# Feed-forward gate and up products computed feature-major, with the weights stationary

## Chip, cores and metric

One core of a Trainium2 chip runs the whole program. The metric is the device time of one execution in microseconds; the profile is one execution taken by the hardware profiler. A difference of 0.2% is about what can be told apart for this kernel.

## What is computed

Two layers of a decoder trunk over x of 256 rows and 1024 features, in float32. Each layer is a token mixer and a feed-forward, each followed by a layer norm. The change touches the feed-forward alone:

```python
def _swiglu(x, w_gate, w_up, w_down):
    hid = jax.nn.silu(jnp.einsum('bsd,df->bsf', x, w_gate)) * jnp.einsum('bsd,df->bsf', x, w_up)
    return jnp.einsum('bsf,fd->bsd', hid, w_down)
```

w_gate and w_up are 1024 x 2816, w_down is 2816 x 1024, one set per layer.

## The kernel before

**Precision.** Every large product is made of three fp32r matmuls: with each operand split into hi (its fp32r rounding) and lo (the rest), a x w is xh*wh + xh*wl + xl*wh. ScalarE casts the hi part, VectorE subtracts for the lo part.

**Weights.** They come as pieces of 128 x 2048 (some smaller) into 3 raw slots by the SP queue (L790); ScalarE casts a piece to one of 5 w_hi slots (L897, step "hi"), VectorE makes w_lo (L1034, step "lo"). The cast of piece i waits until the matmuls of piece i-5 are done; the load of piece i waits for the lo split of piece i-3. A gate-and-up piece holds four blocks of 128 input features, each with 256 columns of w_gate and 256 of w_up side by side. A down piece holds 256 rows of w_down.

**Rows and tiles.** The 256 rows are two tiles t of 128. A matmul has one 128 x 128 stationary operand and one moving operand. In "mm" (L1292 to L1303) the stationary is a block of activations, feature-major (`hi["act"]`, `lo["act"]`, 8 blocks x 256 rows), and the moving operand is the weights, up to 512 columns; the product comes out row-major, in one PSUM bank of 512 columns.

**Order.** `write_plan` writes one list of steps, and each engine runs through the list and issues the steps that concern it, in that order. `mm` puts the splits of coming weight pieces ahead of each step of matmuls: one "lo" step, and one "hi" step for each piece that earlier matmuls have freed.

**Feed-forward.** It has 11 chunks c of 256 hidden features, counted from 0 here. `gate_up` runs, for one tile and one half of the input features, 4 blocks x 3 terms = 12 matmuls of 512 columns: 256 gate columns and 256 up columns. When both halves are done, the step "hidden" takes silu of the gate columns on ScalarE (L1003) and multiplies by the up columns on VectorE (L1140), into `act_fns`. These hidden values are row-major, but as stationary operand of the down product they are needed feature-major. So `turn_hid` transposes them on TensorE, two 128 x 128 blocks per tile (L1312), ScalarE casts the result to `hi["y"]` (L901) and VectorE subtracts for `lo["y"]` (L1041). `down` then runs 2 output halves x 2 blocks x 3 terms = 12 matmuls of 512 columns per tile, accumulated over the chunks in four banks. `y` has 6 block slots, two for each of three chunks.

The order of chunk c for c from 2 to 10: gate and up over input half 0 for both tiles; the two turns of chunk c-1 (for c over 2); input half 1 for both tiles; then, for c up to 8, the down product of chunk c-1. The down products of chunks 8, 9 and 10 come last, tile by tile, and the turns of chunk 10 lie between them (L542 to L549):

```python
for t in range(TT):
    for c in range(FFN_CHUNKS - HELD, FFN_CHUNKS):
        if t == 0 and c > last - TT:
            turn_hid(last, c - last + TT - 1)
```

After them follow the layer norm and the next layer, whose first weight pieces are split meanwhile.

Of the kernel before, what the change touches and what calls it, by code (L numbers as in the profile page):

```python
# [21 lines left out]
F32 = mybir.dt.float32  # L22
F32R = mybir.dt.float32r
I32 = mybir.dt.int32
ALU = mybir.AluOpType
ACT = mybir.ActivationFunctionType

P = 128
# [40 lines left out]
QUARTERS = 4  # L69
STAGES = 2  # L70
FFN_CHUNKS = D_FF // 256


def layer_pieces(layer, w):
# [59 lines left out]
def write_plan(orders, base):  # L134
# [13 lines left out]
    def turn(src, buf, k0, nk, t, dst, dst_k0, ready):  # L148

        use = aux_bank()  # L150
        plan.append(("turn", src, buf, k0, nk, t, dst, dst_k0, use, ready, count.next("turn")))
        return use
# [6 lines left out]
    def split_hi():  # L159
        i = split_next[0]  # L160
        if i < total:
            plan.append(("hi", i, release.get(i - HI_SLOTS)))
            lo_waiting.append(i)
            split_next[0] += 1
# [24 lines left out]
    release = {}  # L189
    attending = [False]  # L190

    def mm(i, t, lhs, outs, frees, lhs_ready, full=()):

        if half_split and half_split[0] <= i:
            finish_lo()
        while lo_waiting and lo_waiting[0] <= i:
            split_lo()
        if attending[0]:
            start_lo()
        else:  # L200
            split_lo()
        if freed[0]:
            freed[0] -= 1
            split_hi()
        plan.append(("mm", i, t, lhs, outs, frees and not full, lhs_ready, full))
        if frees:
            release[i] = ("filled", full[-1]) if full else ("used", count.next("used"))
            freed[0] += 1
# [64 lines left out]
    for layer, order in enumerate(orders):  # L273
# [222 lines left out]
        def gate_up(c, t, half, use, frees):  # L496
            mm(at[("gu", c, half)], t, ("act", ACT_SLOTS[half]), [(use, 0, NW, half == 0, half == 1)],
               frees, turned[t, half], (use,) if half else ())
            if half:
                hid[c, t] = use  # L500
                plan.append(("hidden", c, t, use, count.next("hid")))

        def turn_hid(c, t):
            turned["h", c, t] = turn("hid", c % 2, 0, 2, t, "y", 2 * (c % 3), ("bank", hid[c, t]))

        down_use = {t: None for t in range(TT)}
# [22 lines left out]
        turn_hid(1, 1)  # L529
        for c in range(2, FFN_CHUNKS):  # L530
            use = [gu_bank() for _ in range(TT)]
            for t in range(TT):
                gate_up(c, t, 0, use[t], t == TT - 1)
            if c > 2:
                for t in range(TT):
                    turn_hid(c - 1, t)
            for t in range(TT):
                gate_up(c, t, 1, use[t], t == TT - 1)
            if c < FFN_CHUNKS - HELD + 1:
                for t in range(TT):  # L540
                    down(c - 1, t, t == TT - 1)
# [28 lines left out]
def trunk(nc, d):  # L570
# [9 lines left out]
    with ExitStack() as ctx:  # L580
# [3 lines left out]
        def sem(name):  # L584
            return ctx.enter_context(nc.semaphore(name))
# [92 lines left out]
        exp_done = sem("exp_done")  # L678
        summed = sem("summed")
        silu_done = sem("silu_done")  # L680
        merge_done = sem("merge_done")
        x_ready = sem("x_ready")
        mean_ready = sem("mean_ready")
# [33 lines left out]
        def weights(ring, i, n_rows):  # L717
            _, nk, cols = pieces[i]
            return ring[slot_of(i, n_rows)][:, 0:nk * cols]

        def wait_lo(engine, i):

            engine.wait_ge(lo_done, 2 * (i + 1))
# [150 lines left out]
        def _(act):  # L874
# [10 lines left out]
            for step in PLAN:  # L885
# [60 lines left out]
                elif kind == "scores" and not (step[1]["b"] == 1 and step[1]["t"]) or kind == "scores2":  # L946
                    u = step[1]
                    for e, (b, n) in enumerate(u["s2"] or u["s"]):
                        slot = 2 * (u["u"] % 4) + e
                        pr = prob[u["t"]][e][:, 0:(GROUPS if u["b"] == 1 else 1) * u["w"]]  # L950
                        act.wait_ge(drained[b], n)
                        act.activation(pr, pr, ACT.Exp, bias=neg_max[:, slot:slot + 1], scale=-1.0,  # L952
                                       accum_out=denom[:, slot:slot + 1]).then_inc(exp_done, 1)
                elif kind == "turn_p":
                    u = step[1]
                    b, n = u["pt"]
                    act.wait_ge(filled[b], n)
                    t = u["t"]
                    act.copy(prob_t[:, t:2 * t + 1, :], group_view(bank[b], t + 1, 2 * P)).then_inc(drained[b], 1)
                elif kind == "weigh":  # L960
                    u = step[1]
                    if u["b"] == 1:
                        act.wait_ge(summed, u["sum_n"])
                    act.wait_ge(inverse_done, u["weigh_n"])
                    for e in range(2):
                        slot = 2 * (u["u"] % 4) + e
                        pr = prob[u["t"]][e][:, 0:u["w"]]
                        ins = act.activation(pr, pr, ACT.Identity, scale=rdenom[:, slot:slot + 1])  # L968
                    ins.then_inc(weighed, 1)
                elif kind == "values":  # L970
                    _, u, _, _ = step
                    b, n = u["o"]
                    act.wait_ge(filled[b], n)
                    act.copy(hi["y"][:, Y_SLOTS[u["b"]][u["p"]], :], bank[b][:, 0:SEQ]).then_inc(y_hi_done, 1)
                elif kind == "gate":
                    _, nh, t, (b, n), last_merge = step
                    act.wait_ge(filled[b], n)
                    if last_merge is not None:
                        act.wait_ge(merge_done, last_merge)
                    act.activation(act_fn[2 * nh + t][:, :], bank[b][:, :], ACT.Tanh, scale=0.5).then_inc(drained[b], 1)  # L980
                elif kind == "spread_rows":
                    act.wait_ge(norms_loaded, 16)
                    act.wait_ge(rows_zeroed, 2)
                    act.copy(w_hi[HI_SLOTS - 1][0:4, 0:NW + 4], norm_rows).then_inc(rows_hi_done, 1)
                elif kind == "turn_rows":
                    _, t, k0, nk, (b, n) = step
                    act.wait_ge(filled[b], n)
                    act.copy(merged[t][:, k0 * P:(k0 + nk) * P], bank[b][:, 0:nk * P]).then_inc(drained[b], 1)
                elif kind == "split_rows":
                    t = step[1]  # L990
                    for b, n in first_turns[t]:
                        act.wait_ge(drained[b], n)
                    act.copy(hi["act"][:, :, t * P:(t + 1) * P], group_view(merged[t], KT, P)).then_inc(first_hi, 1)
                elif kind == "statistics":
                    for t, _ in step[1]:
                        means += 1
                        act.wait_ge(mean_ready, means)
                        act.activation(squares_out, x[t][:, :], ACT.Square, bias=neg_mean[:, t:t + 1],  # L998
                                       accum_out=square_sum[:, t:t + 1]).then_inc(squares_ready, 1)
                elif kind == "hidden":  # L1000
                    _, c, t, (b, n), _ = step
                    act.wait_ge(filled[b], n)
                    act.activation(act_fn[2 * (c % 2) + t][:, 0:256], bank[b][:, 0:256],  # L1003
                                   ACT.Silu).then_inc(silu_done, 1)

        @block.vector
        def _(dve):
# [19 lines left out]
            for step in PLAN:  # L1027
# [93 lines left out]
                elif kind == "merge":  # L1121
# [6 lines left out]
                    if br == 0:  # L1128
                        dve.scalar_tensor_tensor(out=out, in0=sig, scalar=1.0, in1=bank[b][:, :],
                                                 op0=ALU.add, op1=ALU.mult).then_inc(drained[b], 1)  # L1130
                    else:
                        dve.scalar_tensor_tensor(out=sig, in0=sig, scalar=1.0, in1=bank[b][:, :],
                                                 op0=ALU.add, op1=ALU.mult).then_inc(drained[b], 1)
                        dve.wait_ge(drained[b], n)
                        dve.tensor_tensor(out, out, sig, ALU.add).then_inc(merge_done, 1)
                elif kind == "hidden":
                    _, c, t, (b, n), idx = step
                    dve.wait_ge(silu_done, idx)
# [96 lines left out]
        def _(pe):  # L1235
# [9 lines left out]
            for step in PLAN:  # L1245
# [36 lines left out]
                if kind == "mm":  # L1282
                    _, i, t, (lhs, slots), outs, frees, (lb, ln), full = step
                    _, nk, cols = pieces[i]
                    pe.wait_ge(first_split if lb == "rows" else drained[lb], ln)
                    wait_lo(pe, i)
                    wh = weights(w_hi, i, HI_SLOTS).rearrange("p (k n) -> p k n", k=nk)
                    wl = weights(w_lo, i, HI_SLOTS).rearrange("p (k n) -> p k n", k=nk)
# [3 lines left out]
                    for o, (use, c0, width, start, stop) in enumerate(outs):  # L1292
# [7 lines left out]
                        if use in full:  # L1300
                            ins.then_inc(filled[use[0]], 1)
                    if frees:
                        ins.then_inc(piece_used, 1)  # L1303
                elif kind == "turn":
                    _, src, buf, k0, nk, t, dst, dk, use, (what, r), idx = step
# [132 lines left out]
```

## Time and profile before

| what | us |
|---|---|
| median of 3 runs | 849.24 (848.91 to 849.33) |
| the profiled execution's own time | 849.19 |
| its span, first to last instruction | 847.3 |
| TensorE matmul busy | 833.9 (98%) |
| TensorE weight load busy | 678.5 (80%) |
| VectorE busy | 484.8 (57%) |
| ScalarE busy | 433.0 (51%) |
| weights and other data moved by DMA | 148.30 MB, mean 175 GB/s |

PE is the matmul side of TensorE and PEld its weight loads, which overlap. Matmuls are pipelined: the duration of one reaches into the next, so the time that one takes in a stream is the distance between starts. DVE is VectorE, ACT ScalarE, SP the queue that issues the transfers. L12 is line 12 of the kernel. An idle time is put down to what released the engine last.

### The profile page before, as it was taken

The numbers are of one execution on the slowest core, as the hardware profiler recorded it, in microseconds if no ns is written. First come the engines' busy times: TensorE is split into PE (matmuls) and PEld (weight loads), VectorE is DVE, ScalarE is ACT, GpSimd is POOL, SyncE is SP. The second block draws the span as 40 slices with busy tenths as digits, with TensorE's granted clock in tenths as the row PEclk, the third lists the DMA queues.
The fourth block names the chain that finished last, engine by engine and source line by source line (L and its number), as shares of the span: only waits on it lengthen the run. The fifth ranks groups of instructions, "written<-read, shape, count | busy, mean of one in ns | idle before, by whom it ended". The sixth has DMA issues, their size and how long they took to land. (4 is left out here: it accounts for less than half of the span.)

```text
span 847.3 us, 10716 instructions
## 1 busy us (share of the span) xinstructions
PE 833.9 (98%) x4125; PEld 678.5 (80%) x4125; DVE 484.8 (57%) x679; ACT 433.0 (51%) x622; POOL 59.2 (7%) x105
## 2 busy tenths in 40 slices
PE   8999999999999999999999999999999999999996
PEld 5887877788878888888888778777888788888885
DVE  7654566475776554455566546563776664455535
ACT  4676666644345344433447676765454544443431
POOL 0022230000000000000000414100000000000000
PEclk9999999999999999999999999999999999999999
DMA  8754443556467566555337543436664586546501
GB/s 299 252 195 135 137 138 125 174 187 235 149 198 251 196 195 196 183 171 199 100 125 249 171 123 104 152 129 214 227 198 137 186 274 199 189 160 198 198 0 50
DMA packets 93497, 148.30 MB, mean 175 GB/s; under 512 B 3460, under 2 KB 54916, under 8 KB 93448
## 3 DMA queue, kind: packets, MB, share of 16 engines
q1 hardware_dynamic: 93448, 147.62, 53.1%
q8 instruction: 34, 0.56, 0.3%
q14 instruction: 15, 0.12, 0.0%
HBM read 146.56 MB, written 1.05 MB: 174 GB/s over the span
## 5 line engine op out<-in xcount | busy, mean ns | idle before, releaser
L1034 DVE TENSOR_TENSOR w_lo<-raw,w_hi 128x2048 fp32r<-128x2048 f32 (+5 forms) x176 | 313.3, 1784 | 114.2 <-ACT w_hi L897 113.4
L1297 PE MATMUL bank<-w_hi,act_hi 128*128 128x512 f32 (+2 forms) x848 | 333.9, 394 | 0.0
L1297 PE MATMUL bank<-w_hi,act_lo 128*128 128x512 f32 (+2 forms) x848 | 324.3, 382 | 0.0
L1297 PE MATMUL bank<-w_lo,act_hi 128*128 128x512 f32 (+2 forms) x848 | 324.0, 382 | 0.0
L897 ACT CAST w_hi<-raw 128x2048 fp32r<-128x2048 f32 (+3 forms) x140 | 253.4, 1812 | 92.6 <-PE bank L1297 81.4
L1297 PEld LDWEIGHTS bank<-w_hi,act_hi 128*128 128x128 f32 x848 | 159.3, 188 | 31.4 <-issue 2.5
L1297 PEld LDWEIGHTS bank<-w_hi,act_lo 128*128 128x128 f32 x848 | 159.2, 188 | 30.8
L1297 PEld LDWEIGHTS bank<-w_lo,act_hi 128*128 128x128 f32 x848 | 159.6, 188 | 27.3 <-issue 0.2
L1297 PE MATMUL bank<-w_hi,y_hi 128*128 128x512 f32 x240 | 94.9, 396 | 0.0
L1297 PE MATMUL bank<-w_hi,y_lo 128*128 128x512 f32 x240 | 93.6, 390 | 0.0
L1297 PE MATMUL bank<-w_lo,y_hi 128*128 128x512 f32 x240 | 93.5, 390 | 0.0
L1297 PEld LDWEIGHTS bank<-w_hi,y_hi 128*128 128x128 f32 x240 | 45.1, 188 | 9.7 <-issue 0.3
L1297 PEld LDWEIGHTS bank<-w_hi,y_lo 128*128 128x128 f32 x240 | 45.1, 188 | 9.6
L1297 PEld LDWEIGHTS bank<-w_lo,y_hi 128*128 128x128 f32 x240 | 45.1, 188 | 8.9
L1140 DVE TENSOR_TENSOR act_fns<-act_fns,bank 128x256 f32<-128x256 f32 x44 | 18.5, 421 | 58.0 <-ACT act_fns L1003 56.3
L901 ACT CAST y_hi<-bank 128x256 fp32r<-128x256 f32 x44 | 14.8, 375 | 69.2 <-PE bank L1312 69.1
L1003 ACT ACTIVATE act_fns<-bank 128x256 f32<-128x256 f32 x44 | 16.9, 384 | 61.1 <-PE bank L1297 61.1
L860 POOL TENSOR_SCALAR var_eps<-square_sum 128x1 f32<-128x1 f32 x8 | 1.5, 190 | 597.1 <-ACT prob_t_squares L998 597.1
L952 ACT ACTIVATE shared<-shared,neg_max 128x128 f32<-128x128 f32 (+3 forms) x64 | 33.8, 529 | 17.7 <-DVE neg_max L1094 10.8
L968 ACT ACTIVATE shared<-shared,rdenom 128x128 f32<-128x128 f32 (+1 forms) x64 | 25.6, 448 | 30.0 <-DVE rdenom L1113 30.0
L1041 DVE TENSOR_TENSOR y_lo<-bank,y_hi 128x256 fp32r<-128x256 f32 x44 | 17.2, 420 | 34.8 <-ACT y_hi L901 34.8
L1049 DVE TENSOR_TENSOR qk_lo<-bank,qk_hi 128x512 fp32r<-128x512 f32 (+1 forms) x24 | 14.4, 601 | 32.3 <-ACT qk_hi L926 32.2
(120 smaller groups left out, 560.8 us busy)
## 6 DMA issues: line engine op xcount, KB each, us to landing
raw<-in_w_in SPq DMA_DIRECT2D x42, 1024.0 KB, 5.1
raw<-in_w_gate SPq DMA_DIRECT2D x44, 512.0 KB, 3.9
raw<-in_w_up SPq DMA_DIRECT2D x44, 512.0 KB, 5.0
raw<-in_w_down SPq DMA_DIRECT2D x22, 1024.0 KB, 4.8
raw<-in_w_o SPq DMA_DIRECT2D x8, 1024.0 KB, 5.3
raw<-in_w_in SPq DMA_DIRECT2D x8, 768.0 KB, 4.4
raw<-in_w_pa SPq DMA_DIRECT2D x4, 768.0 KB, 4.4
raw<-in_w_pc SPq DMA_DIRECT2D x4, 768.0 KB, 4.3
```

What stands on the lines that cost most here:

```text
L860: link(pool.tensor_scalar(var_eps[:, t:t + 1], square_sum[:, t:t + 1], 1.0 / D_MODEL, step[2] * step[2] * LN_EPS, ALU.mult, ALU.add))
L897: act.copy(weights(w_hi, i, HI_SLOTS), weights(raw, i, RAW_SLOTS)).then_inc(hi_done, 1)
L901: act.copy(hi[dst][:, dk:dk + nk, t * P:(t + 1) * P], group_view(bank[b], nk, P)).then_inc(turn_hi, 1)
L952: act.activation(pr, pr, ACT.Exp, bias=neg_max[:, slot:slot + 1], scale=-1.0, accum_out=denom[:, slot:slot + 1]).then_inc(exp_done, 1)
L968: ins = act.activation(pr, pr, ACT.Identity, scale=rdenom[:, slot:slot + 1])
L1003: act.activation(act_fn[2 * (c % 2) + t][:, 0:256], bank[b][:, 0:256], ACT.Silu).then_inc(silu_done, 1)
L1034: dve.tensor_tensor(weights(w_lo, i, HI_SLOTS)[:, cols], weights(raw, i, RAW_SLOTS)[:, cols], weights(w_hi, i, HI_SLOTS)[:, cols].bitcast( ...
L1041: dve.tensor_tensor(lo[dst][:, dk:dk + nk, t * P:(t + 1) * P], full, hi[dst][:, dk:dk + nk, t * P:(t + 1) * P].bitcast(F32), ALU.subtract) ...
L1049: dve.tensor_tensor(qk_lo[ev["g"] % 2][:, pairs, cols], group_view(bank[b], ev["np"], P), qk_hi[ev["g"] % 2][:, pairs, cols].bitcast(F32), ...
L1140: dve.tensor_tensor(a[:, 256:512], a[:, 0:256], bank[b][:, 256:512], ALU.mult).then_inc(drained[b], 1)
L1297: ins = pe.matmul(bank[use[0]][:, 0:width], a, w[:, k, c0:c0 + width], start=start and k == 0 and p == 0, stop=stop and k == nk - 1 and p ...
```

## The change

Chunks 0 and 1 stay as they are. For chunks 2 to 10 `gate_up_turned` takes the place of `gate_up`: the stationary operand is a 128 x 128 block of w_gate or w_up, hi or lo, and the moving operand is the block of activations of both tiles, 256 columns. j counts the two blocks of 128 hidden features. The bank of block j gets gate in columns 0 to 255 and up in columns 256 to 511, feature-major, for both tiles. For one input half and one j there are 4 blocks x 2 parts x 3 terms = 24 matmuls of 256 columns. The step "hidden_turned" takes silu (ScalarE) and product (VectorE), then ScalarE copies the product to `hi["y"]` and VectorE subtracts for `lo["y"]`, both from SBUF. ScalarE waits for VectorE's product between its silu and its copy. `turn_hid` does nothing for these chunks. Both tiles' down products wait for the lo subtraction of block j = 1. `prepare`, the part of `mm` that places the splits of weights, is called as often and at the same places as before.

```diff
--- before.py
+++ after.py
@@ -69,6 +69,7 @@
 QUARTERS = 4
 STAGES = 2
 FFN_CHUNKS = D_FF // 256
+TURNED = 2
 
 
 def layer_pieces(layer, w):
@@ -189,7 +190,7 @@
     release = {}
     attending = [False]
 
-    def mm(i, t, lhs, outs, frees, lhs_ready, full=()):
+    def prepare(i):
 
         if half_split and half_split[0] <= i:
             finish_lo()
@@ -202,6 +203,10 @@
         if freed[0]:
             freed[0] -= 1
             split_hi()
+
+    def mm(i, t, lhs, outs, frees, lhs_ready, full=()):
+
+        prepare(i)
         plan.append(("mm", i, t, lhs, outs, frees and not full, lhs_ready, full))
         if frees:
             release[i] = ("filled", full[-1]) if full else ("used", count.next("used"))
@@ -500,7 +505,22 @@
                 hid[c, t] = use
                 plan.append(("hidden", c, t, use, count.next("hid")))
 
+        def gate_up_turned(c, j, half, use):
+            i = at[("gu", c, half)]
+            prepare(i)
+            plan.append(("mm_turned", i, j, half, use, [turned[t, half] for t in range(TT)]))
+            if j:
+                release[i] = ("filled", use) if half else ("used", count.next("used"))
+                freed[0] += 1
+            if half:
+                hid[c, j] = use
+                plan.append(("hidden_turned", c, j, use, count.next("hid"), count.next("hid_turned")))
+                for t in range(TT):
+                    turned["h", c, t] = ("hid_lo_done", count.n["hid_turned"])
+
         def turn_hid(c, t):
+            if c >= TURNED:
+                return
             turned["h", c, t] = turn("hid", c % 2, 0, 2, t, "y", 2 * (c % 3), ("bank", hid[c, t]))
 
         down_use = {t: None for t in range(TT)}
@@ -529,13 +549,9 @@
         turn_hid(1, 1)
         for c in range(2, FFN_CHUNKS):
             use = [gu_bank() for _ in range(TT)]
-            for t in range(TT):
-                gate_up(c, t, 0, use[t], t == TT - 1)
-            if c > 2:
-                for t in range(TT):
-                    turn_hid(c - 1, t)
-            for t in range(TT):
-                gate_up(c, t, 1, use[t], t == TT - 1)
+            for half in range(2):
+                for j in range(2):
+                    gate_up_turned(c, j, half, use[j])
             if c < FFN_CHUNKS - HELD + 1:
                 for t in range(TT):
                     down(c - 1, t, t == TT - 1)
@@ -678,6 +694,8 @@
         exp_done = sem("exp_done")
         summed = sem("summed")
         silu_done = sem("silu_done")
+        hid_hi_done = sem("hid_hi_done")
+        hid_lo_done = sem("hid_lo_done")
         merge_done = sem("merge_done")
         x_ready = sem("x_ready")
         mean_ready = sem("mean_ready")
@@ -1002,6 +1020,13 @@
                     act.wait_ge(filled[b], n)
                     act.activation(act_fn[2 * (c % 2) + t][:, 0:256], bank[b][:, 0:256],
                                    ACT.Silu).then_inc(silu_done, 1)
+                elif kind == "hidden_turned":
+                    _, c, j, (b, n), _, idx = step
+                    a = act_fn[2 * (c % 2) + j]
+                    act.wait_ge(filled[b], n)
+                    act.activation(a[:, 0:256], bank[b][:, 0:256], ACT.Silu).then_inc(silu_done, 1)
+                    act.wait_ge(drained[b], n)
+                    act.copy(hi["y"][:, 2 * (c % 3) + j, :], a[:, 256:512]).then_inc(hid_hi_done, 1)
 
         @block.vector
         def _(dve):
@@ -1133,6 +1158,16 @@
                                                  op0=ALU.add, op1=ALU.mult).then_inc(drained[b], 1)
                         dve.wait_ge(drained[b], n)
                         dve.tensor_tensor(out, out, sig, ALU.add).then_inc(merge_done, 1)
+                elif kind == "hidden_turned":
+                    _, c, j, (b, n), idx, turned_n = step
+                    a = act_fn[2 * (c % 2) + j]
+                    slot = 2 * (c % 3) + j
+                    dve.wait_ge(silu_done, idx)
+                    dve.tensor_tensor(a[:, 256:512], a[:, 0:256], bank[b][:, 256:512],
+                                      ALU.mult).then_inc(drained[b], 1)
+                    dve.wait_ge(hid_hi_done, turned_n)
+                    dve.tensor_tensor(lo["y"][:, slot, :], a[:, 256:512], hi["y"][:, slot, :].bitcast(F32),
+                                      ALU.subtract).then_inc(hid_lo_done, 1)
                 elif kind == "hidden":
                     _, c, t, (b, n), idx = step
                     dve.wait_ge(silu_done, idx)
@@ -1282,7 +1317,8 @@
                 if kind == "mm":
                     _, i, t, (lhs, slots), outs, frees, (lb, ln), full = step
                     _, nk, cols = pieces[i]
-                    pe.wait_ge(first_split if lb == "rows" else drained[lb], ln)
+                    pe.wait_ge({"rows": first_split, "hid_lo_done": hid_lo_done}[lb] if isinstance(lb, str)
+                               else drained[lb], ln)
                     wait_lo(pe, i)
                     wh = weights(w_hi, i, HI_SLOTS).rearrange("p (k n) -> p k n", k=nk)
                     wl = weights(w_lo, i, HI_SLOTS).rearrange("p (k n) -> p k n", k=nk)
@@ -1300,6 +1336,27 @@
                         if use in full:
                             ins.then_inc(filled[use[0]], 1)
                     if frees:
+                        ins.then_inc(piece_used, 1)
+                elif kind == "mm_turned":
+                    _, i, j, half, use, ready = step
+                    for b, n in ready:
+                        pe.wait_ge(drained[b], n)
+                    wait_lo(pe, i)
+                    wh = weights(w_hi, i, HI_SLOTS).rearrange("p (k n) -> p k n", k=4)
+                    wl = weights(w_lo, i, HI_SLOTS).rearrange("p (k n) -> p k n", k=4)
+                    if half == 0:
+                        take(use)
+                    for k, at_k in enumerate(ACT_SLOTS[half]):
+                        xh, xl = hi["act"][:, at_k, :], lo["act"][:, at_k, :]
+                        for part in range(2):
+                            cols = slice(part * 256 + j * P, part * 256 + (j + 1) * P)
+                            for p, (w, a) in enumerate(((wh, xh), (wh, xl), (wl, xh))):
+                                ins = pe.matmul(bank[use[0]][:, part * 256:(part + 1) * 256], w[:, k, cols], a,
+                                                start=half == 0 and k == 0 and part == 0 and p == 0,
+                                                stop=half == 1 and k == 3 and part == 1 and p == 2)
+                    if half:
+                        ins.then_inc(filled[use[0]], 1)
+                    if j and not half:
                         ins.then_inc(piece_used, 1)
                 elif kind == "turn":
                     _, src, buf, k0, nk, t, dst, dk, use, (what, r), idx = step
```

## Rows read from the trace of the kernel before

**Rows 1.** The page: engines, busy time, share, instructions; TensorE clock by slice.

```profile
PE 833.9 (98%) x4125; PEld 678.5 (80%) x4125; DVE 484.8 (57%) x679; ACT 433.0 (51%) x622; POOL 59.2 (7%) x105
...
PEclk9999999999999999999999999999999999999999
```

**Rows 2.** Waits on TensorE: line <- releaser: us in total, times, longest.

```profile
PE bank L1312 <- DVE x L1228: 1.5, 3, 0.6
PE bank L1249 <- POOL logf_lo L823: 1.3, 1, 1.3
PE bank L1259 <- DVE w_lo L1178: 1.2, 1, 1.2
PE bank L1356 <- issue: 0.9, 1, 0.9
PE bank L1312 <- DVE act_lo L1041: 0.5, 2, 0.3
```

**Rows 3.** Groups by line and form, TensorE: count, then busy us, mean ns.

```profile
L1297 PE MATMUL bank<-w_hi,act_hi 128*128 128x512 f32 x752 | 301.6, 401 | 0.0
...
L1297 PEld LDWEIGHTS bank<-w_hi,act_hi 128*128 128x128 f32 x848 | 159.3, 188 | 31.4 <-issue 2.5 <-DVE qk_lo L1049 0.2
```

**Rows 4.** Timeline of TensorE, a chunk of layer 0: start us, us, line, form.

```profile
357.59 0.60 PE L1312 MATMUL bank<-tables,act_fns 128*128 128x128 f32 x4
...
363.52 0.39 PE L1297 MATMUL bank<-w_hi,y_hi 128*128 128x512 f32 x1
...
374.40 0.60 PE L1312 MATMUL bank<-tables,act_fns 128*128 128x128 f32 x4
```

**Rows 5.** Timeline of TensorE, end of the feed-forward of layer 0.

```profile
411.20 0.38 PE L1312 MATMUL bank<-tables,act_fns 128*128 128x128 f32 x2
...
414.18 0.38 PE L1312 MATMUL bank<-tables,act_fns 128*128 128x128 f32 x2
```

**Rows 6.** Timeline of TensorE, the projections of 262 columns, layers 0 and 1.

```profile
35.23 0.29 PE L1297 MATMUL bank<-w_lo,act_hi 128*128 128x262 f32 x1
...
39.39 0.28 PE L1297 MATMUL bank<-w_hi,act_lo 128*128 128x262 f32 x1
...
448.46 0.28 PE L1297 MATMUL bank<-w_lo,act_hi 128*128 128x262 f32 x1
...
449.20 0.29 PE L1297 MATMUL bank<-w_lo,act_hi 128*128 128x262 f32 x1
...
452.61 0.28 PE L1297 MATMUL bank<-w_hi,act_lo 128*128 128x262 f32 x1
```

**Rows 7.** Timeline of TensorE, a projection of 384 columns, layer 0.

```profile
27.48 0.33 PE L1297 MATMUL bank<-w_hi,act_lo 128*128 128x384 f32 x1
...
30.08 0.34 PE L1297 MATMUL bank<-w_hi,act_lo 128*128 128x384 f32 x1
```

**Rows 8.** Timeline of TensorE, back to 512 columns, layer 1.

```profile
454.42 0.40 PE L1297 MATMUL bank<-w_hi,act_hi 128*128 128x512 f32 x1
...
456.74 0.39 PE L1297 MATMUL bank<-w_lo,act_hi 128*128 128x512 f32 x1
```

**Rows 9.** Groups by line, 300 to 400 us: busy, mean ns, idle before, releaser.

```profile
L1034 DVE TENSOR_TENSOR w_lo<-raw,w_hi 128x2048 fp32r<-128x2048 f32 x19 | 43.5, 2290 | 27.7 <-ACT w_hi L897 27.7
...
L897 ACT CAST w_hi<-raw 128x2048 fp32r<-128x2048 f32 x18 | 34.4, 1912 | 19.9 <-PE bank L1297 19.9
...
L1140 DVE TENSOR_TENSOR act_fns<-act_fns,bank 128x256 f32<-128x256 f32 x12 | 5.1, 421 | 14.0 <-ACT act_fns L1003 13.4
L1003 ACT ACTIVATE act_fns<-bank 128x256 f32<-128x256 f32 x12 | 4.6, 384 | 17.2 <-PE bank L1297 17.2
...
L901 ACT CAST y_hi<-bank 128x256 fp32r<-128x256 f32 x12 | 3.9, 376 | 22.2 <-PE bank L1312 22.2
```

**Rows 10.** Timeline of ScalarE, a hi cast after the second silu of a chunk.

```profile
364.00 1.90 ACT L897 CAST w_hi<-raw 128x2048 fp32r<-128x2048 f32 x1
```

**Rows 11.** Line L1249, warm-up matmuls over one stationary: duration ns min/median/max.

```profile
L1249 PEld LDWEIGHTS bank<-logf_lo,logf_hi x13: 288/330/337, 1.3 to 8.8; 128*128 128x128 f32 x13
```

## Prediction

> **What bounds the kernel now.** I read the page's table of engines and its slices first. The matmul row is busy 98% of the span at a granted clock near 1 in all slices, that is at the 2.4 GHz level [rows 1]. A busy share can hide waits, so I read next who waited for whom on TensorE: five rows, 5.4 us in all, and none belongs to L1297, the line of all large products, or to the transposes of the feed-forward's hidden values [rows 2]. TensorE therefore has no idle time to win in this stretch; its time is the number of matmuls times their spacing. The grouping by form gives a matmul of 512 columns a mean of 401 ns, and a weight load 188 ns [rows 3], but these are durations of overlapping work. The spacing has to be read from start to start, which the timeline gives: from 363.52 us, where the down product of one chunk starts, to 374.40 us, where the next transposes start, there are 48 matmuls of 512 columns in 10.88 us, **226.7 ns** each [rows 4]. 512 columns at 2.4 GHz are 213.3 ns, so a matmul with its load costs 13.4 ns over its streaming.
>
> **The removed part: transposes.** From 357.59 us, where four transposes start, to 363.52 us there are these four and 24 matmuls of 512 columns [rows 4]. The 24 are 5.44 us by the spacing above, the stretch is 5.93 us: four transposes, with the slower restart behind them, cost 0.49 us, not their busy time. Check over one chunk: 374.40 - 357.59 = 16.81 us against 72 x 0.2267 = 16.32 us, again 0.49. Eight such groups per layer go (chunks 2 to 9, counted from 0). Chunk 10 has two groups of two: from 411.20 to 414.18 us lie two transposes and the 12 matmuls of a tile's down product, 2.98 us against 12 x 0.2267 = 2.72 [rows 5], so 0.26 us each. Per layer 8 x 0.49 + 2 x 0.26 = 4.44 us, for two layers **-8.9 us**. All of it is on TensorE, which is never idle there, so all of it counts.
>
> **The changed part: twice the matmuls at half the width.** A gate-and-up chunk was 2 halves x 2 tiles x 4 blocks x 3 terms = 48 matmuls of 512 columns, 48 x 226.7 ns = 10.88 us. Now it is 2 halves x 2 blocks of features x 4 x (gate, up) x 3 = 96 matmuls of 256 columns. The columns streamed are the same; the price of the form is what each matmul costs over its streaming, paid 48 times more. What is that at 256 columns, each with a fresh stationary? Nearest is the projection of 262 columns, the same fp32r form with three terms: 34 intervals from 448.46 to 452.61 us, 4.15 us, 122.1 ns; the later 28 of them, from 449.20, 121.8 ns [rows 6]. Less six columns (2.5 ns) these give 119.6 and 119.3 ns. Two steps of 10 ns rounding over 34 intervals are 0.6 ns, and the like stretch of layer 0, 34 intervals from 35.23 to 39.39 us, gives 122.4 [rows 6], so I take 119.7. At 384 columns 15 intervals are 2.60 us, 173.3 ns, 13.3 over streaming [rows 7], which makes 120.0 at 256: the upper end. So 96 x 0.1197 = 11.49 us, 0.61 us more per chunk, and with 2 x 9 chunks **+11.0 us** (ends 10.3 at 119.3 ns, 11.5 at 120.0).
>
> The weight loads do not bound it: a load lasts 188 ns [rows 3] yet the 262-column matmuls, one load each, start every 122 ns [rows 6]. Were loads one behind another, 96 x 0.188 = 18.0 us per chunk would add 129 us; these rows exclude that. The Trainium skill, page "TensorE: Matmul & The Clock Gate", section "Part 3: Packing small matmuls — row/col tiling", says that a weight load overlaps a running matmul only where the row groups differ; by that rule each of the 864 added loads would stand beside nothing, some 160 us in all, and the trace disagrees with it already at 512 columns, where load and streaming would be 401 ns and are 226.7.
>
> **A small term: going back to 512 columns.** After the 262-column stretch the 512-column matmuls are slower for a while: ten intervals from 454.42 to 456.74 us are 2.32 us instead of 2.27, 0.05 us [rows 8]. In the new order a block of 512-column down products follows a block of 256 columns eight times per layer: 16 x 0.05 = **+0.8 us** (from 0, if that is a matter of the projection's place, to twice that).
>
> **Other engines: nothing on the path, with this cover.** ScalarE and VectorE keep their counts: silu, product, then hi copy and lo subtraction, now from SBUF and behind the product instead of behind a transpose. I cost the copy like the cast from PSUM and the subtraction like its namesake of 421 ns in the timeline [rows 9]. ScalarE gets a new wait: after the silu it stands until VectorE's product. For the first block of a chunk that is 0.4 us. For the second, VectorE may still be in the lo split of a weight piece (2.29 us [rows 9]), put back some 0.85 us by the first block's subtraction; the product ends about 1.6 us after the silu, and the hi cast queued behind it on ScalarE, which in one chunk of before started at 364.00 us [rows 10], starts about 1.7 us later. Its lo split and the SP queue's load into the freed raw slot move with it. The piece is gate and up of two chunks on, first used over 16 us later, and the cast of the piece that takes the reloaded slot waits for TensorE a chunk later; in 100 us of this stretch the casts idle 19.9 us, all of it for TensorE and none for a load [rows 9]. No transfer is added or moved past another. The hi cast of a down piece even starts 0.5 us earlier, since the two casts of transposed values ahead of it are gone.
>
> The tightest place is chunk 10, whose values are used at once. Both blocks must be there before tile 0's down product. After its last matmul: silu (384 ns [rows 9]) by 0.45 us, the product behind a lo split to about 1.5, copy 1.9, subtraction 2.3 us. Between lie the down products of chunks 8 and 9 for tile 0, 24 x 0.2267 = 5.44 us: 3.1 us to spare. If that cover is gone, TensorE waits, with nothing else queued to do.
>
> **Sum.** -8.9 + 11.0 + 0.8 = +2.9 us against the profiled execution's own 849.19 us (span 847.3; the median of the runs is 849.24, the same): **852.1 us**. Ends: 10.3 + 0 - 9.1 = +1.2 (850.4) and 11.5 + 1.6 - 8.7 = +4.4 (853.6), the transposes to 0.01 us a group.
>
> **Rivals.** (A) *The price over streaming is not paid at each new matmul, and it gets faster.* Of three matmuls two use the same hi weights as stationary, in a row; if the 13 ns belong to a new stationary, a third of them drops: mean spacing 115.3 ns, 11.07 us a chunk, +3.4 + 0.8 - 8.9 = -4.7: 844.5 us. It breaks even at 118.0 ns mean spacing, and is faster by over 0.2% under 117.0. Against: where one stationary was used 13 times over, there are 13 loads [rows 11], so none is left out, and at 262, 384 and 512 columns the price is 13 ns alike; for: no row shows a repeated stationary in the flow. The Trainium skill, same page, section "Back-to-back issue gap", gives N/2.4 + 2.5 ns, 109.2 ns at 256 columns; by it the change costs 0.13 us a chunk and the sum is -5.9, 843.3 us. The trace has 226.7 where that rule has 215.8, and 122.1 where it has 111.7, so I give it no more than the mechanism of A: 14% together.
> (B) *A new wait takes the place of the transposes.* At chunk 10, should a cast (1.9) and a further split (2.29) get ahead of the chain, it ends at 6.6 us instead of 2.3, 1.2 us over its cover, in both layers: +2.4, 854.5 us. Against: the planner orders only one split ahead of it, and layer 1 has none left. Instruction supply is of this kind too: 7 matmuls per us instead of 4.6. In the 262-column stretches 8 per us run for 4 us without a gap [rows 6]; over chunks that is not shown. 9%.
> (C) *No difference that can be told* (0.2%, 1.7 us, is about what a measurement of this kernel tells from no change): the low end of the sum, 850.4, does this: spacing 119.3 and no price for going back.
>
> **Chances.** Forecast case 72%: its range 850.4 to 853.6 crosses 850.9, where 0.2% begins, so 60 of it is slower and 12 is C. A 14% (13 faster, 1 within). B 9%, slower. The rest, 5%: 1, 2 and 2. Faster 0.14, within 0.15, slower 0.71. The range 848.0 to 855.0 takes in the forecast case and B, and below it the part of A near its break-even; it leaves out most of A and of the rest.
>
> **What would show it.** TensorE with 792 instructions more (864 added, 72 gone: 4917); the stationary of the chunk's matmuls is w_hi or w_lo, 128x256 moving, start to start 119 to 120 ns; a chunk with its down product 16.93 + 0.05 us instead of 16.81; no wait of the down products on VectorE at chunk 10; ScalarE's and VectorE's busy time the same within a few us. Wrong would be: a spacing under 118 ns or over 121 (each ns is 1.7 us), a spacing that goes by whether the stationary repeats, or a row of TensorE waiting for y_lo.

## The result, and the profile after

The changed kernel takes 851.76 us (median of 7 runs, 851.55 to 852.17) against 849.04 us before (median of 7, 848.77 to 849.33): ratio 1.0033, 95% interval 1.0022 to 1.0044, slower by 2.7 us. The forecast was 852.1 us.

The page of the changed kernel, its engines and the granted TensorE clock by slice:

```profile
PE 836.7 (98%) x4917; PEld 716.5 (84%) x4917; DVE 485.0 (57%) x679; ACT 437.4 (51%) x622; POOL 59.3 (7%) x105
...
PEclk9999999999999999999999999999999999999999
```

Against [rows 1] TensorE has the 792 instructions more that were counted (864 added, 72 gone), at the same clock level. VectorE's busy time is the same, ScalarE's 4 us more. Its 36 copies of 128 x 256 from SBUF took 406 ns each where the casts from PSUM took 376 [rows 9]; that is 1.1 us of it, the rest was not taken apart, and TensorE waits for none of it.

The waits of TensorE in the changed kernel (line <- releaser: us in total, times, longest):

```profile
PE bank L1369 <- DVE x L1263: 1.5, 3, 0.6
PE bank L1284 <- POOL logf_lo L841: 1.3, 1, 1.3
PE bank L1294 <- DVE w_lo L1213: 1.2, 1, 1.2
PE bank L1413 <- issue: 0.8, 1, 0.8
PE bank L1369 <- DVE act_lo L1066: 0.5, 2, 0.3
```

It is the list of before [rows 2] under other line numbers. The new matmuls (L1354) and the down products (L1333) wait for nothing, so the 2.7 us are work of TensorE, to be read from starts. The timeline of TensorE around one steady chunk, from down product to down product:

```profile
347.80 0.40 PE L1333 MATMUL bank<-w_hi,y_hi 128*128 128x512 f32 x1
...
353.26 0.28 PE L1354 MATMUL bank<-act_hi,w_hi 128*128 128x256 f32 x1
...
364.78 0.40 PE L1333 MATMUL bank<-w_hi,y_hi 128*128 128x512 f32 x1
...
370.24 0.28 PE L1354 MATMUL bank<-act_hi,w_hi 128*128 128x256 f32 x1
```

From 353.26 to 364.78 us lie the 96 matmuls of 256 columns: 11.52 us, **120.0 ns** each. From 364.78 to 370.24 lie the 24 down matmuls: 5.46 us where 24 x 226.7 ns are 5.44. The chunk is 16.98 us, 0.17 more than the 16.81 of before [rows 4].

The end of layer 0, where the last chunk's values are used at once. First TensorE, then VectorE, in the changed kernel:

```profile
410.26 0.40 PE L1333 MATMUL bank<-w_hi,y_hi 128*128 128x512 f32 x1
...
423.89 0.60 PE L1369 MATMUL bank<-tables,x 128*128 128x128 f32 x4
```

```profile
409.23 2.28 DVE L1059 TENSOR_TENSOR w_lo<-raw,w_hi 128x2048 fp32r<-128x2048 f32 x1
411.43 0.41 DVE L1166 TENSOR_TENSOR act_fns<-act_fns,bank 128x256 f32<-128x256 f32 x1
412.32 0.42 DVE L1169 TENSOR_TENSOR y_lo<-act_fns,y_hi 128x256 fp32r<-128x256 f32 x1 [0.47 <-ACT y_hi L1029]
```

The product of the second block stands behind the lo split, as was foreseen, and y_lo is there at 412.74 us, 2.5 us after the down products of chunk 8 began at 410.26. They and those of chunk 9 hold TensorE for 5.4 us: 2.9 us to spare (forecast 3.1). From 410.26 to 423.89 us, 60 down matmuls run without a gap.

### The profile page after: what moved, and what is told of

It is laid out like the page before. It is cut to its first block and busy times, and to the rows that moved or that the text cites. A ratio compares the mean times of both kernels' runs of the same rounds, so it can differ in the third digit from the quotient of the medians.

```text
span 850.1 us, 12300 instructions
## 1 busy us (share of the span) xinstructions
PE 836.7 (98%) x4917; PEld 716.5 (84%) x4917; DVE 485.0 (57%) x679; ACT 437.4 (51%) x622; POOL 59.3 (7%) x105
## 5 line engine op out<-in xcount | busy, mean ns | idle before, releaser
L1333 PE MATMUL bank<-w_hi,act_hi 128*128 128x512 f32 (+2 forms) x560 | 220.1, 393 | 0.0
L1333 PE MATMUL bank<-w_hi,act_lo 128*128 128x512 f32 (+2 forms) x560 | 212.0, 379 | 0.0
L1333 PE MATMUL bank<-w_lo,act_hi 128*128 128x512 f32 (+2 forms) x560 | 211.7, 378 | 0.0
L1354 PE MATMUL bank<-act_hi,w_hi 128*128 128x256 f32 x576 | 163.1, 283 | 0.0
L1354 PE MATMUL bank<-act_hi,w_lo 128*128 128x256 f32 x576 | 163.0, 283 | 0.0
L1354 PE MATMUL bank<-act_lo,w_hi 128*128 128x256 f32 x576 | 163.0, 283 | 0.0
L1333 PEld LDWEIGHTS bank<-w_hi,act_hi 128*128 128x128 f32 x560 | 105.2, 188 | 20.7 <-issue 2.5
L1333 PEld LDWEIGHTS bank<-w_hi,act_lo 128*128 128x128 f32 x560 | 105.1, 188 | 19.3
L1333 PEld LDWEIGHTS bank<-w_lo,act_hi 128*128 128x128 f32 x560 | 105.4, 188 | 16.5 <-issue 0.2
L1354 PEld LDWEIGHTS bank<-act_lo,w_hi 128*128 128x128 f32 x576 | 110.5, 192 | 0.5
L1354 PEld LDWEIGHTS bank<-act_hi,w_hi 128*128 128x128 f32 x576 | 110.5, 192 | 0.6
L1354 PEld LDWEIGHTS bank<-act_hi,w_lo 128*128 128x128 f32 x576 | 110.5, 192 | 0.0
L1333 PE MATMUL bank<-w_hi,y_hi 128*128 128x512 f32 x240 | 94.8, 395 | 0.0
L1333 PE MATMUL bank<-w_lo,y_hi 128*128 128x512 f32 x240 | 93.7, 390 | 0.0
L1333 PE MATMUL bank<-w_hi,y_lo 128*128 128x512 f32 x240 | 93.5, 390 | 0.0
L1333 PEld LDWEIGHTS bank<-w_hi,y_lo 128*128 128x128 f32 x240 | 45.1, 188 | 9.6
L1333 PEld LDWEIGHTS bank<-w_hi,y_hi 128*128 128x128 f32 x240 | 45.1, 188 | 9.4 <-issue 0.3
L1333 PEld LDWEIGHTS bank<-w_lo,y_hi 128*128 128x128 f32 x240 | 45.2, 188 | 8.5
```

The costliest lines, as they stand in the source:

```text
L1333: ins = pe.matmul(bank[use[0]][:, 0:width], a, w[:, k, c0:c0 + width], start=start and k == 0 and p == 0, stop=stop and k == nk - 1 and p ...
L1354: ins = pe.matmul(bank[use[0]][:, part * 256:(part + 1) * 256], w[:, k, cols], a, start=half == 0 and k == 0 and part == 0 and p == 0, sto ...
```

## The experiments

The theory: TensorE is never idle in the feed-forward, each matmul costs its columns at 2.4 GHz and 13.3 ns, a group of four transposes 0.49 us, and the change is the difference of the two. Times stand beside runs of the kernel before on the same chip (medians 848.8 to 849.0 us).

**The transposes alone.** In the kernel before, `turn_hid` returns for chunks 2 to 10:

```diff
         def turn_hid(c, t):
+            if c >= 2:
+                turned["h", c, t] = hid[c, t]
+                return
```

> The kernel before, with the transposes, hi casts and lo subtractions of the hidden values of chunks 2 to 10 left out (72 transposes of 128 columns on TensorE; the down products read what was in y before). Theory (each group of four transposes costs 0.49 us of TensorE's time, restart included, and all of it counts): 8.9 us less than before, 840.1 us, and the groups' gaps in the spacing of 226.7 ns are gone. Rival (the transposes were hidden in part and some other wait appears in their place): 3 to 6 us less, 843 to 846, with a wait on TensorE in the list.

Measured: 840.05 us, 8.8 us less (ratio 0.9896, interval 0.9881 to 0.9911). The forecast term was 8.9. TensorE's timeline for one chunk of it:

```profile
284.83 0.39 PE L1300 MATMUL bank<-w_hi,act_hi 128*128 128x512 f32 x1
...
295.71 0.39 PE L1300 MATMUL bank<-w_hi,y_hi 128*128 128x512 f32 x1
```

48 matmuls in 10.88 us: the 226.7 ns again, with no wait in place of what was taken out.

**The number of matmuls alone, row-major.** In the kernel before, activations stay stationary and the transposes stay, but each matmul of gate and up of chunks 2 to 10 becomes two of 256 columns:

```diff
+                            for part in range(2):
+                                cols = slice(part * 256, (part + 1) * 256)
+                                for p, (a, w) in enumerate(((xh, wh), (xh, wl), (xl, wh))):
+                                    ins = pe.matmul(bank[use[0]][:, cols], a, w[:, k, cols],
```

> The kernel before, still row-major and with its transposes, but gate and up of chunks 2 to 10 in two matmuls of 256 columns in place of one of 512 (activations stationary, 864 matmuls more). Theory (the cost is the number of matmuls at 13.3 ns each over streaming, whichever operand is stationary): 18 x 48 x 13.3 ns = 11.5 us more than before plus up to 0.5 for going back to 512 columns, 860.5 to 861.0 us, start to start 120.0 ns. Rival (it is the new orientation, weights as stationary, that costs): spacing nearer 113 ns, 849 to 855 us.

Measured: 861.21 us, 12.4 more than before (ratio 1.0149, interval 1.0133 to 1.0164). In its timeline of TensorE, one chunk with its down product, the transposes within:

```profile
284.94 0.28 PE L1302 MATMUL bank<-w_hi,act_hi 128*128 128x256 f32 x1
...
290.70 0.60 PE L1328 MATMUL bank<-tables,act_fns 128*128 128x128 f32 x4
...
302.36 0.28 PE L1302 MATMUL bank<-w_hi,act_hi 128*128 128x256 f32 x1
```

The first 48 matmuls take 5.76 us, 120.0 ns each, the same as with the weights stationary: the orientation costs nothing by itself. The chunk is 302.36 - 284.94 = 17.42 us against 16.81 [rows 4], 0.61 more, and 18 x 0.61 = 11.0 us. It is a little under 0.64 because the restart after the transposes is cheaper with narrow matmuls: the 48 behind them take 5.84 us, 0.08 over 5.76, where the 24 wide ones of before took some 0.12 over 5.44. The other 1.4 us lie outside these chunks and were not explained; this profiled execution has 1.9 us of waits of TensorE in lines outside the feed-forward that the kernel before does not show, and no term is made of them.

**Does a repeated stationary cost less?** Two kernels, the changed one with another order of the three terms (first line added), and with one term replaced so that each stationary comes three times in a row (second line added):

```diff
-for p, (w, a) in enumerate(((wh, xh), (wh, xl), (wl, xh))):
+for p, (w, a) in enumerate(((wh, xh), (wl, xh), (wh, xl))):
+for p, (w, a) in enumerate(((wh, xh), (wh, xl), (wh, xh))):
```

> The changed kernel with the three terms in the order wh*xh, wl*xh, wh*xl, so that no two matmuls in a row have the same stationary operand. Theory (each matmul pays, whether its stationary is new or not): 851.8 us, as the changed kernel, spacing 120.0 ns. Rival A (a repeated stationary costs less than a new one, and the changed kernel already had some of that): slower, up to 7.7 us, 859 us.

> The changed kernel with wh*xh, wh*xl and again wh*xh, so that three matmuls in a row have one stationary operand (the term with the lo weights is left out of gate and up, one with the hi weights computed twice). Theory: spacing 120.0 ns, 851.8 us. Rival A (a repeated stationary is free of the 13.3 ns): 32 more of the 96 matmuls of each chunk without the price, spacing about 115.6, 844 us.

Measured: 851.73 us (ratio to before 1.0035, interval 1.0022 to 1.0047) and, one run, 851.83 us, both the changed kernel's time. The timelines of one chunk, first without repeats:

```profile
284.93 0.28 PE L1354 MATMUL bank<-act_hi,w_hi 128*128 128x256 f32 x1
...
296.44 0.40 PE L1333 MATMUL bank<-w_hi,y_hi 128*128 128x512 f32 x1
```

then with repeats only:

```profile
285.14 0.28 PE L1354 MATMUL bank<-act_hi,w_hi 128*128 128x256 f32 x1
...
296.65 0.40 PE L1333 MATMUL bank<-w_hi,y_hi 128*128 128x512 f32 x1
```

11.51 us in both. Rival A is out: each matmul brings its own load (4917 loads for 4917 matmuls in both kernels) and pays alike.

**Fewer matmuls for the same columns.** If it is the count that costs, hi and lo activations side by side let one matmul with w_hi as stationary stream 512 columns. ScalarE and VectorE then add two halves of a bank:

```diff
+        act_pair = sb("act_pair", [P, KT, 2, SEQ], F32R)
...
+                            pe.matmul(out[:, :], wh[:, k, cols], act_pair[:, at_k, :, :],
+                                      start=half == 0 and k == 0, stop=False)
+                            ins = pe.matmul(out[:, 0:SEQ], wl[:, k, cols], hi["act"][:, at_k, :],
+                                            start=False, stop=half == 1 and k == 3)
```

> The changed kernel with hi and lo activations side by side in one buffer, so that one matmul of 512 columns with a block of w_hi as stationary does wh*xh and wh*xl (into the two halves of a bank, one bank for gate and one for up), and one of 256 columns adds wl*xh to the first half: 64 matmuls per chunk in place of 96, the same columns. ScalarE and VectorE add the halves (2 copies and 2 additions more per block of features). Theory (the cost is the count of matmuls at 13.3 ns): 18 x 32 x 13.3 ns = 7.7 us less than the changed kernel, 844.1 us, some 5 us below the kernel before, a chunk's gate and up in 11.1 us; at most 0.5 us of it lost where chunk 10 needs the banks of chunk 9 drained. Rival 1 (switching between widths costs, as after the transposes: up to 3 to 7 ns on each matmul of 512 columns): 32 x 5 ns x 18 = 2.9 us of it lost, 847 us. Rival 2 (the additions on VectorE and ScalarE hold up the banks or the hidden values): a wait of TensorE in the list, 849 us or more.

Measured: 848.2 us (ratio 0.9992, interval 0.9983 to 1.0001), 3.6 us less than the changed kernel and no more than even with the kernel before. Of the 7.7 us expected, half is missing. Its timeline of TensorE:

```profile
301.60 0.28 PE L1365 MATMUL bank<-act_pair,w_lo 128*128 128x256 f32 x1
301.72 0.40 PE L1363 MATMUL bank<-act_pair,w_hi 128*128 128x512 f32 x1
301.95 0.28 PE L1365 MATMUL bank<-act_pair,w_lo 128*128 128x256 f32 x1
...
305.96 0.40 PE L1363 MATMUL bank<-act_pair,w_hi 128*128 128x512 f32 x1
```

From 301.72 to 305.96 us are 12 pairs, 353 ns each, where 226.7 + 120.0 make 346.7: 6.6 ns a pair too much. One chunk does not pay this. It is chunk 2 of layer 0, the first of all, with the same order of widths:

```profile
268.37 0.40 PE L1363 MATMUL bank<-act_pair,w_hi 128*128 128x512 f32 x1
...
278.77 0.40 PE L1363 MATMUL bank<-act_pair,w_hi 128*128 128x512 f32 x1
```

These are 30 pairs in 10.40 us, 346.7 ns each. In the other 17 chunks a pair takes 353 ns; 544 pairs at 6.6 ns are 3.6 us, and with the down products behind them, which take 5.50 us instead of 5.46, that is the missing half. Rival 1 named the price, at the upper end of its range, but changing the width is not enough to bring it on, and what chunk 2 of layer 0 has that the others lack is open.

**Is there a floor below 256 columns?** The changed kernel, each matmul split by tile into two of 128 columns:

```diff
+                                for t in range(TT):
+                                    c0 = part * 256 + t * P
+                                    ins = pe.matmul(bank[use[0]][:, c0:c0 + P], w[:, k, cols], a[:, t * P:(t + 1) * P],
```

> The changed kernel with each matmul of gate and up of chunks 2 to 10 split once more, one per tile, 192 matmuls of 128 columns per chunk. Theory (13.3 ns over streaming at any width): 192 x 66.7 ns = 12.8 us per chunk, 18 x 96 x 13.3 ns = 23 us more than the changed kernel, 874.8 us. Rival (at some width the weight load bounds the spacing; with loads of 188 ns that overlap, it would show as a spacing well over 66.7 ns): at 120 ns each, 18 x 192 x 53 ns = 184 us more.

Measured, one run: 1031.12 us, 179 us more than the changed kernel. The theory as it stood fell here. The timeline of one chunk:

```profile
295.21 0.33 PE L1356 MATMUL bank<-act_hi,w_hi 128*128 128x128 f32 x2
...
316.60 0.45 PE L1333 MATMUL bank<-w_hi,y_hi 128*128 128x512 f32 x1
```

192 matmuls in 21.39 us, **111.4 ns** each, where 53.3 + 13.3 were expected: half the columns take nearly the time of 256. So there is a floor on the time of a matmul with its load. A last kernel of this kind asks whether it holds at a width between:

```diff
-ins = pe.matmul(bank[use[0]][:, part * 256:(part + 1) * 256], w[:, k, cols], a,
+ins = pe.matmul(bank[use[0]][:, part * 256:part * 256 + 192], w[:, k, cols], a[:, 0:192],
```

> The changed kernel with 192 of the 256 columns in each matmul of gate and up of chunks 2 to 10 (the products of the last 64 rows are left out there). e6_128_columns took 21.4 us for 192 matmuls of 128 columns, 111.4 ns each. Theory now (a stream of fresh weight blocks has a floor of 111 to 112 ns a load, and columns/2.4 GHz + 13.3 ns bounds only above it): 96 x 111.5 ns = 10.7 us per chunk, 18 x 0.8 = 14.7 us less than the changed kernel, 837.1 us. Rival (13.3 ns over streaming at 192 columns too, and the floor has to do with the split by tiles): 96 x 93.3 ns, 46 us less, 806 us.

Measured, one run: 837.1 us. The timeline of one chunk of it:

```profile
284.14 0.25 PE L1354 MATMUL bank<-act_hi,w_hi 128*128 128x192 f32 x1
...
294.84 0.41 PE L1333 MATMUL bank<-w_hi,y_hi 128*128 128x512 f32 x1
```

96 matmuls in 10.70 us, 111.5 ns. With 128 or 192 columns the time is the same, with 256 it is 120.0, with 384 and 512 columns it is columns plus 13.3. The change stopped 8 ns above the floor.

Is it the load that sets the floor? No kernel was built to separate the two, but a short stretch of the kernel before speaks for it. First its weight loads, then its matmuls:

```profile
49.52 0.19 PEld L1334 LDWEIGHTS bank<-upper_r,logf_hi 128*128 128x128 f32 x1
49.64 0.19 PEld L1334 LDWEIGHTS bank<-upper_r,logf_lo 128*128 128x128 f32 x1
49.75 0.19 PEld L1297 LDWEIGHTS bank<-w_hi,act_hi 128*128 128x128 f32 x1
```

```profile
49.64 0.22 PE L1334 MATMUL bank<-upper_r,logf_hi 128*128 128x128 f32 x1
49.70 0.28 PE L1334 MATMUL bank<-upper_r,logf_lo 128*128 128x128 f32 x1
```

The two matmuls of 128 columns start 0.06 us apart, so such a matmul can follow another in well under 111 ns; the loads start 0.11 to 0.12 us apart. A kernel whose stationary blocks have fewer columns would settle it. If it is the loads, the same spacing prices the transposes, as an estimate: 4 x 111.5 ns make 0.45 of the 0.49 us of a group of four, and 2 x 111.5 ns make 0.22 of the 0.26 us of a group of two.

The Trainium skill, page "TensorE: Matmul & The Clock Gate", section "LDWEIGHTS (loading the stationary operand)", gives a load the number of its columns over 1.2 GHz, 106.7 ns for 128; the floor measured here is 111.5 ns, 5 ns more, so the rule comes near if the floor is that of the load. The row's 188 ns for a load [rows 3] is a duration, and the loads overlap: at 111.5 ns from start to start it is not the price of one.

**The pairs in another order.** Within each half of a chunk, 16 wide matmuls in a row and 16 narrow ones:

```diff
+                groups = [[(512, 0), (512, 1)], [(256, 0), (256, 1)]][j] if half == 0 else \
+                    [[(256, 0), (256, 1), (512, 0)], [(512, 1)]][j]
```

> e5_paired with its matmuls in another order: within each input half of a chunk 16 of 512 columns and 16 of 256 in a row (in the second half the narrow ones first), so that the width goes up once per chunk and not 32 times. In e5_paired a pair of 512 and 256 columns took 353 ns where its two spacings, 226.7 and 120.0, make 346.7. Theory (a matmul of 512 columns behind narrower ones costs some 6 ns more, and only there): 18 x 32 x 346.7 ns with 0.03 to 0.05 us per chunk for the one step up, 3.2 to 3.6 us less than e5_paired, 844.5 to 845.0 us, 0.5% below the kernel before. Rival (the 6 ns belong to the form, two halves of one bank written at once, not to the order): 848.2 us again, each matmul of 512 columns 233 ns apart in its run. Rival 2 (hidden values come later, both blocks near the end of the chunk): a wait of TensorE for a bank or for y_lo at chunk 10, 846 to 848 us.

Measured: 851.72 us (ratio 1.0033, interval 1.0021 to 1.0044; its seven runs spread from 849.72 to 852.79), 3.5 us more than with alternating widths. Yet its steady chunks are as the theory has them, in TensorE's timeline:

```profile
285.45 3.79 PE L1370 MATMUL bank<-act_pair,w_hi 128*128 128x512 f32 x16
289.07 4.00 PE L1367 MATMUL bank<-act_pair,w_lo 128*128 128x256 f32 x32
292.90 3.82 PE L1370 MATMUL bank<-act_pair,w_hi 128*128 128x512 f32 x16
296.56 0.39 PE L1344 MATMUL bank<-w_hi,y_hi 128*128 128x512 f32 x1
```

285.45 to 296.56 us is 11.11 us, against 11.52 in the changed kernel; 16 wide ones behind narrow ones take 3.66 us where 16 x 226.7 ns are 3.63. So the extra 6.6 ns do not belong to the form, two halves of one bank written at once: they come with alternating widths (though not in every chunk, as shown above) and are gone in long runs. The waits of TensorE in this kernel show the first of the losses (one row of the list), and its timeline between chunks 9 and 10 where it is:

```profile
PE bank L1370 <- DVE act_fns L1174: 3.6, 2, 1.8
```

```profile
399.68 2.09 PE L1370 MATMUL bank<-act_pair,w_hi 128*128 128x512 f32 x8 [1.83 <-DVE act_fns L1174]
```

and VectorE's timeline just before:

```profile
396.59 2.28 DVE L1065 TENSOR_TENSOR w_lo<-raw,w_hi 128x2048 fp32r<-128x2048 f32 x1
398.79 0.74 DVE L1174 TENSOR_TENSOR act_fns<-act_fns,bank 128x256 f32<-128x256 f32 x2
```

Each chunk holds four banks, and between chunks 9 and 10 no down product lies in which they could be drained: the additions that drain them stand behind a lo split. Rival 2 had the mechanism, but the time came out above its 846 to 848 us. Layer 0 lost about 3.0 us at three places (2.1 there, 0.6 at the first such chunk, 0.3 at chunk 10's down product) of the 3.9 us that nine chunks gained. The rest of the loss in this kernel, 1.3 us of the profiled execution, lies outside these stretches and was not taken apart.

**Both forms, each where it fits.** Chunks 3 to 9 grouped, chunks 2 and 10 in the form of the changed kernel:

```diff
+GROUPED = range(3, 10)
...
+            if c not in GROUPED:
+                groups = [(0, j)]
```

> e7_grouped for chunks 3 to 9, chunks 2 and 10 in the form of the changed kernel (one bank per block of features, 96 matmuls of 256 columns). In e7_grouped a steady chunk with its down product took 16.55 us (16.98 in the changed kernel), and the time was lost at three places: TensorE waited 1.8 us per layer for banks of chunk 9 whose additions stood behind a lo split of 2.29 us, 0.4 us for the banks of chunk 1's transposes, 0.3 us for y_lo at chunk 10. Theory (these waits alone ate the gain): 2 x 7 x 0.43 = 6.0 us less than the changed kernel, 845.7 us, no wait of TensorE for act_fns or y_lo, 0.4% below the kernel before. Rival (VectorE's additional work delays the splits of the next layer too): waits stay, 848 us or more.

Measured: 845.97 us, ratio **0.9964**, interval 0.9950 to 0.9977: 3.0 us faster than the kernel before, 5.8 faster than the changed kernel. TensorE waits for neither act_fns nor y_lo, and a chunk is, in its timeline,

```profile
296.29 0.39 PE L1368 MATMUL bank<-w_hi,y_hi 128*128 128x512 f32 x1
...
312.84 0.39 PE L1368 MATMUL bank<-w_hi,y_hi 128*128 128x512 f32 x1
```

16.55 us against 16.98 and 16.81 [rows 4]. This is the version to keep: it has the gain of the missing transposes (8.8 us) and pays about half of what the narrow matmuls cost (14 chunks at 0.23 us and 4 at 0.64, 5.8 us in place of 11.5).

## Why the prediction was right, point by point

- *The bound.* TensorE without idle time, to be costed by starts: shown. The changed kernel, e1_no_transposes and e8_192_columns moved by what their matmuls and transposes make, to 0.3 us. In e2_row_major_256 that holds within the chunks, and 1.4 us outside them are unexplained.
- *Transposes, -8.9 us.* Measured by themselves: -8.8.
- *Spacing 119.7 ns at 256 columns, +11.0 us.* It is 120.0, the value from the 384-column rows [rows 7] that stood as the upper end; 18 x 0.64 = 11.5. The 262-column rows [rows 6] had given 0.3 ns less, which is within the rounding of two starts over 34 intervals.
- *Going back to 512 columns, +0.8 us.* In the place itself 5.46 us instead of 5.44, 0.02 to 0.03 us sixteen times, 0.4 us. Half of the term that [rows 8] gave. This error and the one before it cancel, which is luck: the sum is nearer than its two terms.
- *Sum.* 11.5 + 0.4 - 8.9 = +3.0; the medians differ by 2.7, the spans by 2.8.
- *"The weight loads do not bound it."* True at 256 columns, but the reason given (loads overlap, as 188 is more than 122) only excluded loads one behind another at their full duration. There is a floor of 111.5 ns, for which the prediction had no term, and 256 columns lie just above it. At 192 columns its price of 13.3 ns over streaming would have failed.
- *The other engines.* ScalarE stood for VectorE's product as described (1.04 us at chunk 10's second block, behind the split), nothing waited for it, and the spare time there was 2.9 us for 3.1. A copy costs 406 ns, not 376, without effect.
- *Rival A* (a repeated stationary is cheaper): refuted by two kernels. The rule that went with it, of the Trainium skill, page "TensorE: Matmul & The Clock Gate", section "Back-to-back issue gap", stays disagreed with here: 120.0 ns measured at 256 columns, 109.2 by columns over 2.4 GHz plus 2.5 ns. The section gives it for isolated matmuls, without a budget for weight loads. *Rival B* (a new wait): not in the changed kernel, but waits of this kind are what spoiled e7_grouped. Its sum in the prediction is slightly off: 2.3 + 1.9 + 2.29 is 6.5 us and not 6.6, so +2.1 us for both layers and not +2.4; nothing else hangs on it. *C*: the effect is clear of noise.

## What to carry to other kernels

Where TensorE is never idle, cost an edit by distances between starts, and look for rows of the same form at several widths: here columns over 2.4 GHz plus 13.3 ns down to 256 columns. A layout that saves transposes by making matmuls narrower pays that price once per added matmul, so count both: 4 transposes in a group (0.49 us) are worth some 37 added matmuls, and this change added 48. The way out was to keep the layout and widen the moving operand again, two terms with one stationary side by side, in long runs of one width and only where a stretch of other work drains the banks.

## What the runs showed of the hardware

- A matmul with a fresh or a repeated 128 x 128 fp32r stationary has a floor of 111.4 to 111.5 ns between starts in a long stream, at 128 and at 192 columns. That the load sets it is argued and not tested.
- Where matmuls of 512 and 256 columns alternate, a pair costs 6.6 ns more than its two spacings (353 ns against 346.7) in 17 of 18 chunks, and nothing more in one; the reason for the difference is open. Before a run of 16 or 24 wide ones the step up costs 0.02 to 0.03 us in all.
- Which operand is stationary, weights or activations, and whether it repeats, makes no difference that the rows show (11.51 or 11.52 us per 96 matmuls in each).
